# Finer weight pieces for two more chunks, another order on ScalarE in the beginning, halved square sums, and another split of the second block's value and mixing work

## The reference

```python
hx = modulate(rmsnorm(x, norm1_g), mx[0], mx[1])      # shift, scale from silu(c) @ ada_w
hc = modulate(rmsnorm(ctx, norm1_g), mc[0], mc[1])    # the same for 256 context tokens
ux, uc = hx @ w_in, hc @ w_in                         # w_in: 1024 x 5120
# gated linear recurrence, both directions; the context's final states start that of x
# Fourier mixing, gates, w_a, w_b, w_out; then norm, ffn_up, 3x3 convolution, ffn_down
# second block:
p = rms_norm(x, norm1_g_2) @ w_in_2                   # q, k, v, conv gates, pool input
y_attn = chunked_band_attention(rms_norm(q), rms_norm(k), v, rel_bias)
y_conv = gb * causal_conv3(gc * hin)                  # 256 features
y_pool = multiscale_pool(u)                           # 256 features
x = x + concat(y_attn, y_conv, y_pool) @ w_out_2
x = x + square(relu(rms_norm(x) @ w_mlp1)) @ w_mlp2
```

## Time and profile before

| | us |
|---|---|
| median of 3 runs (lowest, highest) | 764.88 (763.89, 765.9) |
| the profiled execution's own time | 764.52 |
| its span | 762.5 |
| TensorE busy in the span | 739.1 (97%) |
| weight loads of TensorE (beside its products) | 717.0 (94%) |
| DVE, POOL, ACT busy | 491.2, 398.5, 358.6 |

### The profile page before, as it was taken

How to read it: one execution, slowest core, us unless ns; L and a number is a source line. 1 busy time by engine, 2 the same in 40 slices (tenths; PEclk the granted TensorE clock), 3 DMA queues, 4 the chain that set the end, 5 groups by cost and what they waited for, 6 DMA issues and landing times.

```text
span 762.5 us, 14142 instructions
## 1 busy us (share of the span) xinstructions
PE 739.1 (97%) x5852; PEld 717.0 (94%) x5852; DVE 491.2 (64%) x907; ACT 358.6 (47%) x452; POOL 398.5 (52%) x223
## 2 busy tenths in 40 slices
PE   7779999999999989999999999999899999999998
PEld 3679889999999989999999999999899999999997
DVE  3877797569526559777777764548655656556553
ACT  5586224245434555554555546346454433334331
POOL 0767553546648957878878877766585300000000
PEclk9999999999999989999999999999999999999999
DMA  9984886337534437555455544433435464464411
GB/s 362 417 360 162 344 304 262 140 111 244 207 110 159 166 117 294 177 188 200 167 170 199 184 167 166 166 112 111 148 133 203 181 220 165 169 216 160 176 57 56
DMA packets 21089, 145.84 MB, mean 191 GB/s; under 512 B 2465, under 2 KB 2977, under 8 KB 3746
## 3 DMA queue, kind: packets, MB, share of 16 engines
q1 hardware_dynamic: 20880, 144.87, 51.8%
q10 hardware_dynamic: 146, 0.07, 0.0%
HBM read 143.88 MB, written 1.05 MB: 190 GB/s over the span
## 4 chain that ended last, share of the span: by engine, by line
PE 90%; DVE 4%; ACT 4%; issue 2%; DMA 0%; DVEq 0%; ACTq 0%
PE bank L1426 24%; PE bank L1428 24%; PE bank L1427 24%; PE bank L1444 3%; PE CP L1428 2%; PE CP L1426 2%; PE CP L1427 2%; PE bank L1533 2%; PE bank L1469 1%; ACT SCR L793 1%; ACT whi L487 1%; PE bank L1484 1%; DVE GA L1119 1%; PE CP L1458 0%; PE bank L1642 0%
## 5 line engine op out<-in xcount | busy, mean ns | idle before, releaser
L469 POOL TENSOR_TENSOR wlo<-raw,whi 128x512 fp32r<-128x512 f32 (+1 forms) x201 | 377.8, 1910 | 170.6 <-ACT whi L487 170.5
L487 ACT ACTIVATE whi<-raw 128x2048 fp32r<-128x2048 f32 x103 | 196.3, 1907 | 43.7 <-PE bank L1428 29.2
L1186 DVE SCALAR_TENSOR_TENSOR Y<-bank,vec,Y 128x189 f32<-128x189 f32 (+2 forms) x352 | 123.0, 423 | 43.6 <-ACT Y L734 43.6
L1426 PE MATMUL bank<-H2h,whi 128*128 128x256 f32 x352 | 101.0, 287 | 1.7 <-DVE H2l L1161 1.7
L1427 PE MATMUL bank<-H2l,whi 128*128 128x256 f32 x352 | 100.6, 286 | 0.0
L1428 PE MATMUL bank<-H2h,wlo 128*128 128x256 f32 x352 | 99.8, 284 | 0.0
L1426 PE MATMUL bank<-H1h,whi 128*128 128x256 f32 (+1 forms) x288 | 90.9, 316 | 8.3 <-DVE H1l L917 4.5
L1428 PE MATMUL bank<-H1h,wlo 128*128 128x256 f32 (+1 forms) x288 | 89.2, 310 | 0.0
L1427 PE MATMUL bank<-H1l,whi 128*128 128x256 f32 (+1 forms) x288 | 89.0, 309 | 0.0
L850 DVE TENSOR_TENSOR wlo<-raw,whi 128x2048 fp32r<-128x2048 f32 x28 | 64.4, 2300 | 34.5 <-ACT whi L487 34.5
L1426 PE MATMUL bank<-H4h,whi 128*128 128x256 f32 x256 | 72.6, 284 | 0.0
(11 more groups left out here) (326 smaller groups left out, 1878.9 us busy)
## 6 DMA issues: line engine op xcount, KB each, us to landing
raw<-in_w_mlp SPq DMA_DIRECT2D x32, 1024.0 KB, 4.8
raw<-in_w_in SPq DMA_DIRECT2D x30, 1024.0 KB, 5.7
raw<-in_ffn_up SPq DMA_DIRECT2D x22, 1024.0 KB, 4.9
raw<-in_ada_hi SPq DMA_DIRECT2D x16, 1024.0 KB, 4.9
raw<-in_ffn_down SPq DMA_DIRECT2D x11, 1024.0 KB, 4.8
raw<-in_w_out SPq DMA_DIRECT2D x8, 1024.0 KB, 4.8
ada_s<-in_ada_s SPq DMA_DIRECT2D x4, 1024.0 KB, 18.1
ada_p<-in_ada_p SPq DMA_DIRECT2D x2, 1024.0 KB, 10.2
```

What stands on the lines that cost most here:

```text
L469: m = e.tensor_tensor(l[:, a:a + step], r[:, a:a + step], h[:, a:a + step].bitcast(F32), ALU.subtract)
L487: e.activation(whi[q % NHI][:, :], raw[n % NRAW][:, :], ACT.Copy).then_inc(s["w_hi"], 1)
L1186: e.scalar_tensor_tensor(o[:, r0:r1, c0:c1], z[:, r0 + dr:r1 + dr, c0 + dc:c1 + dc], cw[:, f, tap:tap + 1], o[:, r0:r1, c0:c1], ALU.mult, ...
L1426: e.matmul(out, h[:, col:col + P], xh, start=first, stop=False, skip_group_check=True)
```

## The change

- `FINE` is 6, so chunks 4 and 5 of `w_in` are split in halves and quarters too, and TensorE runs them with `first`.
- ACT's order in the beginning is another: the first half of chunk 4 comes before the second token squares and the second half after them, chunk 5 comes right after the root, all four first scales come after both chunks, and the split of chunk 6, `high(6)`, comes after the last context tile. Single scales and shifts wait for their own dot product only.
- DVE adds the squares of x in pairs of tiles, and TensorE sums four tiles instead of eight. DVE does the context's dot products of `ada_s` 1 ahead of the context's reciprocal, and those of `ada_s` 2 ahead of the context's first tiles.
- In the second block ACT makes `VV`, directly behind the splits and copies that stand there, and DVE no longer does. The convolution's high and low parts come last, and `order2` takes them last.
- `fu_done` and `sg_done` become one semaphore.

```diff
-FINE = 4
+FINE = 6
...
-                e.wait_ge(s[f"raw{q}"], 16)
+                n = place[split[q]]
+                e.wait_ge(s[f"raw{n % NRAW}"], 16 * (n // NRAW + 1))
...
         def scales(x, i, dots):
             e.wait_ge(s["lb_step"], 9)
-            e.wait_ge(s["ada_dot"], dots)
             for k in (2 * i, 2 * i + 1):
+                e.wait_ge(s["ada_dot"], dots - 1 + k % 2)
...
+        project_evict("w_in", 1, flat(Q[:, 2:4, :]), ACT.Silu, "q_done")
+        first_high(4, 0)
         token_squares(1)
-        project_evict("w_in", 1, flat(Q[:, 2:4, :]), ACT.Silu, "q_done")
-        project_evict("w_in", 2, flat(FU[:, 0:2, :]), ACT.Copy, "fu_done")
+        first_high(4, 1)
         warm(ACT.Sqrt)
         e.wait_ge(s["sq_in"], 6)
         e.activation(RC[:, 2:4], RC[:, 2:4], ACT.Sqrt, bias=eps[:, 0:1], scale=1.0 / D).then_inc(s["rms_in"], 1)
-        high(4)
+        project_evict("w_in", 2, flat(FU[:, 0:2, :]), ACT.Copy, "fu_sg")
+        first_high(5, 0)
+        first_high(5, 1)
         shifts(1, 2, 14)
         shifts(1, 3, 16)
         scales(1, 0, 18)
-        high(5)
         scales(1, 1, 20)
-        input_high(1, range(0, 4))
-        project_evict("w_in", 3, flat(FU[:, 2:4, :]), ACT.Copy, "fu_done")
+        input_high(1, range(0, 2))
+        project_evict("w_in", 3, flat(FU[:, 2:4, :]), ACT.Copy, "fu_sg")
+        input_high(1, range(2, 4))
         scales(1, 2, 22)
         input_high(1, (4, 5))
+        scales(1, 3, 24)
+        input_high(1, (6, 7))
         high(6)
-        scales(1, 3, 24)
         for n in range(2):
             e.activation(CP[:, n * 512:n * 512 + 512], CB[:, n * 512:n * 512 + 512], ACT.Copy).then_inc(s["cx_row"], 1)
...
-        input_high(1, (6, 7))
...
+        def values_2(i):
+            two_ = slice(2 * (i - 8), 2 * (i - 8) + 2)
+            e.wait_ge(s["gemm"], starts["w_in_2", i] + 1)
+            for t in range(2):
+                e.activation(VV[:, t, two_, :], product("w_in_2", i)[:, t * T:(t + 1) * T].rearrange(
+                    "p (f c) -> p f c", f=2), ACT.Identity, scale=RC[:, 2 + t:3 + t]).then_inc(s["val_2"], 1)
+
         turn_probabilities(0)
-        e.wait_ge(s["conv_2"], 8)
-        e.activation(MXh[:, 4:6, :], YC[:, :, :], ACT.Copy).then_inc(s["mix_hi"], 1)
         high(turn["w_in_2", 9] + 2)
+        values_2(8)
         turn_probabilities(1)
+        values_2(9)
         for tp in range(2):
             e.wait_ge(s["av"], tp + 1)
             e.activation(MXh[:, 2 * tp:2 * tp + 2, :], two(bank[misc_bank[f"av{tp}"]][:, :]),
                          ACT.Copy).then_inc(s["mix_hi"], 1)
+        e.wait_ge(s["conv_2"], 8)
+        e.activation(MXh[:, 4:6, :], YC[:, :, :], ACT.Copy).then_inc(s["mix_hi"], 1)
...
+        for n in range(2):
+            e.wait_ge(s["sq_in"], 2 * n + 2)
+            e.tensor_tensor(SQI[:, 4 * n:4 * n + 2, :], SQI[:, 4 * n:4 * n + 2, :], SQI[:, 4 * n + 2:4 * n + 4, :],
+                            ALU.add).then_inc(s["sq_add"], 1)
         ada_rows("ada_s", 0, 0)
...
         ada_rows("ada_s", 0, 1)
+        ada_rows("ada_s", 1, 1)
         reciprocal(2, 2, ("rms_in", 2), "rstd_in")
-        ada_rows("ada_s", 1, 1)
+        ada_rows("ada_s", 2, 1)
         input_tiles(1, CX, rc, range(0, 4))
-        ada_rows("ada_s", 2, 1)
         input_tiles(1, CX, rc, (4, 5))
         ada_rows("ada_s", 3, 1)
...
-        mix_low(YC[:, :, :], 4, 2)
-        values_2(8)
-        values_2(9)
         for tp in range(2):
-            mix_low(two(bank[misc_bank[f"av{tp}"]][:, :]), 2 * tp, 3 + tp)
+            mix_low(two(bank[misc_bank[f"av{tp}"]][:, :]), 2 * tp, 2 + tp)
+        mix_low(YC[:, :, :], 4, 4)
...
-            for k in range(KT):
-                if k % 2 == 0:
-                    e.wait_ge(s["sq_in"], k // 2 + 1)
-                m = e.matmul(bank[5][:, 0:T], ones[:, 0:P], SQI[:, k, :], start=k == 0, stop=k == KT - 1)
+            for k in (0, 1, 4, 5):
+                if k % 4 == 0:
+                    e.wait_ge(s["sq_add"], k // 4 + 1)
+                m = e.matmul(bank[5][:, 0:T], ones[:, 0:P], SQI[:, k, :], start=k == 0, stop=k == 5)
...
-                pair("w_in", i, hx, hl)
+                first(i, range(0, 8), group("w_in", i))
...
-            n = {3: 1, 2: 2, 0: 3, 1: 4}[k // 2]
+            n = {3: 1, 0: 2, 1: 3, 2: 4}[k // 2]
...
-        order2 = [6, 7, 4, 5, 0, 1, 2, 3]
+        order2 = [6, 7, 0, 1, 2, 3, 4, 5]
```

More of the change, by code:

```diff
@@ L101, in product_tables @@
         if name == "w_in":
-            e = ([("q_done", i + 1)] if i < 2 else [("fu_done", i - 1)] if i < 4 else [("sg_done", i - 3)] if i < 6 else
+            e = ([("q_done", i + 1)] if i < 2 else [("fu_sg", i - 1)] if i < 6 else
                  [("one_minus", 2 * i - 11), ("one_minus", 2 * i - 10)] if i < 10 else
@@ L135 @@
 MISC2 += [(f"pt{n}", "pt_done", n + 1) for n in range(6)]
-MISC2 += [(f"av{n}", "mix_lo", n + 3) for n in range(2)] + [("col3", "rms_x", 2), ("rows3", "rr_done", 3)]
+MISC2 += [(f"av{n}", "mix_lo", n + 2) for n in range(2)] + [("col3", "rms_x", 2), ("rows3", "rr_done", 3)]
 def misc_tables():
@@ L159 @@
 ada_t3 ada_p0 ada_p1 stores ones_set lb_step lb_exp c_spread c_silu cx_row ada_dot ada_row
-shift_row shift_t shift_pe shift_in scale_in sq_in sum_in rms_in
+shift_row shift_t shift_pe shift_in scale_in sq_in sq_add sum_in rms_in
 rstd_in row_in h1_mul h1_hi h1_lo w_hi lo_pool lo_dve gemm q_done f_sig f_gate v_done edges one_minus scan k_ctx qf ks ctx_t
@@ L163 @@
 wide_out o_mm on_done on_sq rdo_col rdo_rms rdo_rstd rdo_row
-rdo_gain rdo_norm yh_hi yh_lo fu_done sg_done ga_done gb_done gate_a gate_b merged mg_hi mg_lo side mods x1 sq1
+rdo_gain rdo_norm yh_hi yh_lo fu_sg ga_done gb_done gate_a gate_b merged mg_hi mg_lo side mods x1 sq1
 sq1_sum h2_mul h2_hi h2_lo mid conv silu gate a_hi a_lo x2 h3_hi sq2 h3_lo col2 rstd2 rms2 rr_done proj qk_sq qk_col
@@ L643, in scalar @@
                 e.wait_ge(s["rms_in"], 2)
-                project_evict("w_in", i, flat(SG[:, 2 * (i - 4):2 * (i - 4) + 2, :]), ACT.Silu, "sg_done")
+                project_evict("w_in", i, flat(SG[:, 2 * (i - 4):2 * (i - 4) + 2, :]), ACT.Silu, "fu_sg")
             elif i < 10:
@@ L1095, in vector @@
         gate_a(0)
-        e.wait_ge(s["sg_done"], 2)
+        e.wait_ge(s["fu_sg"], 4)
         e.wait_ge(s["on_sq"], 2)
@@ L1240, in project_in @@
                             RR[:, :].unsqueeze(1).to_broadcast([P, 2, T]), ALU.mult).then_inc(s["proj"], 1)
[L1242 to L1248, removed]
         def qk_rstd(i):
@@ L1626, in tensor @@
                 e.wait_ge(s["vec2_in"], 48)
-                e.wait_ge(s["fu_done"], 2)
+                e.wait_ge(s["fu_sg"], 2)
                 for t in range(2):
```

## The result

The changed kernel takes 766.5 us in the median (765.47 to 767.45), the kernel before 764.9 in the same series. The ratio is 1.0017, with a 95% interval of 1.0011 to 1.0022: slower by 1.3 us (the medians differ by 1.6), clear of noise and inside the bound of 0.3%. One of the twenty executions of the kernel before took 943.3 us and is left out of the ratio. The profiled execution took 766.55 us, its span is 764.7 for 762.5.

A forecast was written before the change was run, and what follows sets the result against it. TensorE, busy 97% of the span, was taken to bound the kernel, with chunk 6's start deciding. 764.52 + 2.6 (weights) + 1.3 (clock) - 1.8 (second block) = 766.6, taken as 766.8 us; range 763.4 to 768.9.

The forecast's parts named there:

- Chunk 6's weights (+2.6): First block: chunk 6's split comes behind the context tiles, so chunk 6 starts at 71.6 for 69.03, +2.6 us.
- the drain that the prediction set against it: ACT's table change before the context's root: by the skill's notes the root would come some 1.3 us later; 1.4 kept.
- Clock (+1.3): Behind the new idle time of 5.9 us ahead of chunk 6: a low clock on the path, +1.3 us.
- the rival of the longer low clock: At chunk 6, behind the new wait: low clock costs 3.4 us for 1.3, 768.7 us in all; chance 0.26.
- Second block (-1.8): Attention products behind chunk 9: TensorE starts at 544.1, -1.8 us, with a wait for ACT of 0.9 us left.
- Square sums (0): Beginning: 1.6 us saved at the end of the sums doesn't outlast the token rows' landing; nothing at the end.
- The low clock in chunks 4 and 5 (0): At 56 to 60 us: cost 1.7 us, but POOL's 68.93 was the limit as well, so its going brings nothing.
- Sum: Whole kernel: 766.6 us on the profiled execution's time, taken as 766.8; a small loss inside the bound of 0.3%.
- the three rivals: Longer low clock, 768.7 us (0.26); chunk 6's weights not late, 762.3 (0.12); nothing in the second block, 768.4 (0.08).

The follow-up runs named there:

- high6_early: The changed kernel with chunk 6's split on ACT moved ahead of the last two context tiles: 760.59 us, 0.9936 to the kernel before.
- fill: The changed kernel with 40 additional products of no use ahead of the end of chunk 5: 764.85 us, 0.9997 to the kernel before.
- first_only: The changed kernel with the second block's lines of the diff undone: 769.01 us, 1.0056 to the kernel before.
- root_early: The changed kernel with second token squares, table change and root ahead of both halves of chunk 4: 765.15 us, 1.0000 to the kernel before.
- second_only: The kernel before with the second block's part of the change alone: 763.24 us, 0.9976 to the kernel before.
- values_dve: The changed kernel with the second block's values scaled on DVE again, behind the convolution: 770.55 us, 1.0066 to the kernel before.
- squares_whole: The changed kernel without DVE's additions, TensorE summing eight tiles of squares again: 766.79 us, 1.0019 to the kernel before.
- before_fill: The kernel before with 28 additional products of no use between chunks 3 and 4: 764.74 us, 1.0003 to the kernel before.
- seven_late_root: The changed kernel with chunk 6's split ahead of the last two context tiles and chunk 6 in halves and quarters: 759.58 us, 0.9934 to before.

## Why the prediction was right, step by step

**Chunk 6's weights (+2.6).** Right in place and size. The split was said to start at 64.5 and started at 64.46, POOL 66.5 and 66.44, chunk 6 71.6 and 71.50: +2.5 us. The stations on the way agree within 0.2 us: the root (50.7 for 50.91), first context scale (54.1 for 54.21), first multiply:

```profile
54.72 0.88 DVE L925 SCALAR_TENSOR_TENSOR bank<-CX,A,bank 128x256 f32<-128x256 f32 x2 [0.98 <-ACT A L537]
...
61.75 1.22 DVE L911 CUSTOM_DVE_ANT_0 ada_s<-ada_s,CP 128x1024 f32<-128x1024 f32 x1
```

at 54.72 for 54.6. The table change takes 1.40 us to the root (49.51 to 50.91), as in the rows; the drain that the prediction set against it isn't there. high6_early shows the cause by taking it away.

**Clock (+1.3).** Right: fill puts 1.5 us on it. The traces agree: from chunk 6's start to the second block's last transposes the changed kernel takes 468.54 us (71.50 to 540.04), the kernel before 467.00 (69.03 to 536.03), with as much low clock at 270 us in both. The trace of the changed kernel shows 2.6 us of low clock from 72 to 76 us (0.32 x 4 / 0.5), and the half microsecond of chunk 6 ahead of it was low too (its first product takes 0.77 us for 0.47): 3.1 us, half of it lost, 1.5. The same wait in first_only has a longer fall,

```profile
68.00:72.00 4.00, 0.65 (x2) 0.58 (x3) 3.91 (x8) 3.41 (x4) 4.00 (x4) 0.76 0.00 0
72.00:76.00 4.00, 4.00 (x11) 3.13 (x10) 0.00 (x0) 0.00 (x0) 4.00 (x4) 0.50 0.74 262
76.00:80.00 4.00, 4.00 (x17) 3.18 (x17) 0.00 (x0) 3.47 (x3) 1.98 (x3) 0.89 0.67 225
```

low from about 70.1 to 76.9 us (0.24, 0.50 and 0.11 x 4 / 0.5 in the three windows), of which 5.5 us lie behind chunk 6's start at 71.35: 2.8 us lost. root_early's is as long (0.50 and 0.34 x 4 / 0.5, until 74.7), with 2.4 us lost behind 69.99. That is the rival of the longer low clock. It is there in single executions, though the windows overstate it a little: from chunk 6's start to the transposes ahead of those above, first_only takes 461.64 us and root_early 461.37 for 459.31 in fill, which is 2.3 and 2.1 us more. fill, which compares medians, puts the usual price at 1.5.

**Second block (-1.8).** Right: second_only gives 1.8, and TensorE's wait is 0.97 us for the 0.9 foretold. The order on ACT alone doesn't do it, as values_dve shows; the values' move alone wasn't run.

**Square sums (0).** Right in the end. Their own size was misjudged (1.0 us at their end, not 1.6), which nothing hung on: squares_whole. The 0.73 us a tile was a mean of two speeds. Before, nine records fall in the 4 us from 8.00, one every 0.43 us, and the last ones stand 0.22 us apart, as products of as many columns do behind them (19 from 12.30 to 16.30). All eight of the changed kernel stand 0.43 us apart or more, so four tiles take 3.78 us and not 2.9. By its pace that is the low level of the clock; the windows show 1.00 there because the traces have no record of the clock ahead of 12.3 us (13.1 in the changed kernel). In squares_whole the sixteen records take 5.12 us and end at 12.97, so in that execution the halving is worth 0.1 us.

**The low clock in chunks 4 and 5 (0).** Right for the profiled execution, and before_fill's median agrees. It isn't so in every execution of this beginning. In second_only, which begins as the kernel before, the clock is low for 3.4 us between 24 and 32 us (0.96 and 0.61) and for 6.8 between 52 and 64 (0.88, 0.50 and 0.77). The token squares start at 42.30 for 41.37, POOL has chunk 6's low part at 69.85, and TensorE starts chunk 6 without a wait at 70.54, 1.5 us late. The kernel before's own times fit: of its 21 executions in that series, the seven with a granted clock of 0.993 take 763.8 to 764.5 us, the four with 0.989 take 765.9 to 766.2.

**Sum.** 766.8 was said and 766.5 measured; by the ratio the loss is 1.3 us where 2.1 was worked out on the profiled execution, whose span shows 2.2. The profiled executions are single ones, and what the low clock costs differs from one to the next (1.5 to 2.8 us above), so a difference of under 1 us between a sum from one trace and a median isn't to be explained further. The base was a low one too: the earlier trace rows come from an execution with one short fall ahead of chunk 6, and second_only and the times above show that there are others. The stretch at 270 us adds to the scatter: it is 6.8 us low in the executions shown of the kernel before and of the changed one and 3.4 in fill's, first_only's and root_early's, and from chunk 6's start to the transposes at 529.08 us (530.93 in fill) that makes 0.7 us, 460.05 for 459.31. Of the three rivals none was the rule.

The prediction left out one fall of the clock: the changed kernel has 0.84 from 24 to 28 us and 0.73 from 28 to 32, 3.4 us low, where the profiled execution of the kernel before has full clock. second_only has it too, so it comes with the execution and not with the change. In the changed kernel ACT waits 1.46 us for the token squares' landing all the same and chunk 3 begins by that, so nothing of it reaches the end.

## What to carry to other kernels

Where two chains meet at one instruction, saving on one of them gives nothing, and making room for it at the cost of the other loses: read which wait ends last at the meeting, here POOL's low part, and follow its list back before touching anything. An item on an engine's list belongs into a stretch in which that engine waits anyway; one line moved there was worth about 6 us. And a wait of TensorE's may cost more than its own length, by the low clock behind it.

## What the runs showed of the hardware

- **Useless products can pay.** 40 of them in an idle stretch of 5.7 us kept the clock at 2.4 GHz and gave 1.5 us; the Trainium skill (TensorE: Matmul & The Clock Gate, section "HAM oscillation — how this bites in real kernels") warns of long gaps, and the runs agree for the longest: each of 5.7 and 6.4 us had a fall behind it. Shorter ones go either way, with the execution and not with the kernel: the wait of 2.6 us ahead of the rows had none behind it in the changed kernel and one in seven_late_root and high6_early, and that of 1.9 us at 24 us one in the changed kernel and in second_only and none in the kernel before.
- **POOL's earlier work lengthened DVE's.** In the second block the split of the next weights comes earlier, so POOL goes straight on to them, and the same four instructions of DVE's convolution take 5.71 us for 3.74, its last multiply 1.64 for 0.69. Before:

```profile
537.53 3.74 DVE L1321 SCALAR_TENSOR_TENSOR YC<-Z,vec,YC 128x255 f32<-128x255 f32 x4
541.31 0.69 DVE L1362 TENSOR_TENSOR YC<-YC,PP 128x512 f32<-128x512 f32 x1
```

After, DVE and then POOL, whose twelve pieces take 1.62 us each for the 1.26 of the earlier trace rows (the eight of this stage before take 13.49 us, 1.69 each, and end at 540.07):

```profile
541.55 5.71 DVE L1330 SCALAR_TENSOR_TENSOR YC<-Z,vec,YC 128x255 f32<-128x255 f32 x4
547.29 1.64 DVE L1371 TENSOR_TENSOR YC<-YC,PP 128x512 f32<-128x512 f32 x1
```

```profile
530.59 19.47 POOL L469 TENSOR_TENSOR wlo<-raw,whi 128x512 fp32r<-128x512 f32 x12 [7.11 <-ACT whi L487]
```

Of the four before, the two that run beside POOL take 1.40 and 1.51 us and the two behind its end 0.48 each; after, all four take 1.40 to 1.52. The Trainium skill (SBUF — State Buffer, section "SBUF: two separate sides") says that DVE, with both its inputs in SBUF, and GpSimd share a pair of ports and exclude each other. The trace agrees, both being slower where they run together, and DVE's multiply of 128 x 512 with one input in PSUM (529.28 us, before) takes 0.69 us beside POOL. I hadn't reckoned with it. It was hidden, since the convolution comes last. In values_dve, where the values wait for the convolution, it isn't: DVE ends it 8.8 us behind the start of the transposes, for 6.0 in the kernel before. That this makes values_dve so dear is worked out from these rows; no run takes it away.
